# Two-tap filter in the first layer of a block compressor, with the prompt queries kept in DRAM meanwhile

## The reference

```python
CMP_BLOCK = 32; CMP_STRIDE = 16; CMP_HIDDEN = 128; HD_B = 64; N_KV_B = 2

def compress_blocks(kv, pe, w1, w2):
    B, L = kv.shape[:2]
    nseg = L // CMP_STRIDE
    r = CMP_BLOCK // CMP_STRIDE
    n_cmp = nseg - r + 1
    segs = kv[:, :nseg * CMP_STRIDE].reshape(B, nseg, CMP_STRIDE, 2, N_KV_B, HD_B)
    blocks = jnp.concatenate([segs[:, j:j + n_cmp] for j in range(r)], axis=2)
    blocks = blocks + pe.transpose(1, 0, 2)[:, :, None, :]
    flat = blocks.transpose(0, 1, 3, 4, 2, 5).reshape(B, n_cmp, 2, N_KV_B, CMP_BLOCK * HD_B)
    hid = jax.nn.gelu(jnp.einsum('bnkgf,kfh->bnkgh', flat, w1))
    return jnp.einsum('bnkgh,khd->bnkgd', hid, w2)
```

## Time and profile before

| | |
|---|---|
| median of 3 runs | 2916.55 us (2914.92 to 2917.1) |
| profiled execution | 2917.17 us, its span 2915.4 us |
| PE busy | 2804.9 us (96%), 21195 matmul records |
| PE weight loads busy | 2672.6 us (92%) |
| DVE busy | 1190.1 us (41%) |
| ACT busy | 625.0 us (21%) |
| POOL busy | 1008.8 us (35%) |
| mean granted PE clock | 0.986 |

### The profile page before, as it was taken

One profiled execution on the slowest core, in us unless ns is written; L12 is line 12 of the kernel. 1 busy time (PEld: TensorE's weight loads), 2 busy tenths in 40 slices (PEclk: granted clock), 3 DMA queues, 4 the chain that ended last, 5 costly groups with the idle time before them and its releaser, 6 DMA issues.

```text
span 2915.4 us, 49271 instructions
## 1 busy us (share of the span) xinstructions
PE 2804.9 (96%) x21195; PEld 2672.6 (92%) x21195; DVE 1190.1 (41%) x1244; ACT 625.0 (21%) x1092; POOL 1008.8 (35%) x484
## 2 busy tenths in 40 slices
PE   7999989999898799999999999999999999999998
PEld 7999878876776599999999999999999999999998
DVE  5121273345543215444334444416335434444345
ACT  4100044546665302000110001211111110001102
POOL 6342100100002444444344444533554434444340
PEclk9999999989999899999999999999999999999999
DMA  5111243200103531111111111311211111111111
GB/s 182 45 45 49 87 138 94 90 31 2 74 2 131 174 109 44 51 44 44 50 43 50 43 45 48 123 38 50 93 39 52 44 51 43 47 46 43 50 50 58
DMA packets 204235, 185.46 MB, mean 64 GB/s; under 512 B 8013, under 2 KB 185426, under 8 KB 202362
## 3 DMA queue, kind: packets, MB, share of 16 engines
q1 hardware_dynamic: 193290, 160.28, 17.6%
q0 software_dynamic: 4608, 16.78, 1.5%
q10 hardware_dynamic: 6192, 6.29, 0.8%
HBM read 162.41 MB, written 25.09 MB: 64 GB/s over the span
## 4 chain that ended last, share of the span: by engine, by line
PE 79%; issue 8%; DVE 6%; ACT 2%; POOL 2%; DMA 2%; SPq 0%; POOLq 0%; DVEq 0%; ACTq 0%
PE psum L266 49%; PE psum L476 6%; PE psum L298 5%; PE psum L1484 4%; PE psum L1890 2%; PE psum L286 2%; DVE xlo L338 2%; PE psum L1864 2%; POOL whl L237 1%; PE psum L1827 1%; PE psum L1468 1%; DMA wrow<-in_state_win_kv 1%; POOL whl L240 1%; DVE nmax L1993 1%; PE psum L313 1%
## 5 line engine op out<-in xcount | busy, mean ns | idle before, releaser
L266 PE MATMUL psum<-xhi,whl 128*128 128x344 f32 x4656 | 864.0, 320 | 1.3 <-ACT vCs L692 0.6
L237 POOL TENSOR_TENSOR whl<-wraw,zeroc 128x1024 fp32r<-128x1024 f32 x186 | 372.9, 2005 | 1172.2 <-PE psum L266 815.1
L266 PEld LDWEIGHTS psum<-xhi,whl 128*128 128x128 f32 x4656 | 756.2, 188 | 2.3 <-issue 2.1
L240 POOL TENSOR_TENSOR whl<-wraw,whl 128x1024 fp32r<-128x1024 f32 x186 | 501.6, 2697 | 14.6
L266 PE MATMUL psum<-xlo,whl 128*128 128x344 f32 x2328 | 494.1, 321 | 0.0
L266 PE MATMUL psum<-ahi,whl 128*128 128x344 f32 x2304 | 427.5, 320 | 0.2
L266 PEld LDWEIGHTS psum<-xlo,whl 128*128 128x128 f32 x2328 | 394.1, 189 | 0.0
L266 PEld LDWEIGHTS psum<-ahi,whl 128*128 128x128 f32 x2304 | 373.2, 188 | 4.4 <-DVE ftmp L558 3.7
L545 DVE CAST ahi<-frel 128x1032 fp32r<-128x1032 f32 x64 | 170.7, 2667 | 476.3 <-ACT frel L522 475.8
L520 ACT ACTIVATE frel<-psum 128x1032 f32<-128x1032 f32 x64 | 66.1, 1033 | 1231.9 <-PE psum L266 1190.0
L558 DVE TENSOR_TENSOR ftmp<-psum,fscale 128x1032 f32<-128x1032 f32 x127 | 156.3, 1231 | 307.7 <-PE psum L266 247.3
(11 more groups left out here) (430 smaller groups left out, 3062.7 us busy)
## 6 DMA issues: line engine op xcount, KB each, us to landing
wraw<-in_w_ffn SPq DMA_DIRECT2D x128, 512.0 KB, 3.8
rows<-in_cache_cmp_kv SPq DMA_DIRECT2D x128, 128.0 KB, 2.5
wraw<-in_w_in_ab SPq DMA_DIRECT2D x26, 512.0 KB, 3.7
hT<-h_spill SPq DMA_DIRECT2D x8, 1032.0 KB, 8.1
wraw<-in_w_in_c SPq DMA_DIRECT2D x16, 512.0 KB, 3.9
h_spill<-hT SPq DMA_DIRECT2D x4, 1032.0 KB, 8.3
h_spill<-hT SPq DMA_DIRECT2D x1, 4128.0 KB, 12.9
wrow<-in_state_win_kv SPq DMA_DIRECT2D x4, 1024.0 KB
```

Source lines behind the costliest of these rows:

```text
L237: pool.tensor_tensor(whl[:, s, 0, :], raw, zeroc[:, 0:1].to_broadcast([P, UNIT]), ALU.add).then_inc(w_hi, 1)
L240: pool.tensor_tensor(whl[:, s, 1, :], raw, whl[:, s, 0, :].bitcast(F32), ALU.subtract).then_inc(w_ready, 1)
L266: last = pe.matmul(psum[:, 3 * bset + c, 0:TC], w, rhs[ah][:, k0 + k, c * TC:(c + 1) * TC], start=(k == 0 and n == 0), stop=(k == kn - 1 a ...
```

## The change

Pair the blocks. With e[m] = x[2m], o[m] = x[2m+1], block 2m is A e[m] + B o[m] and block 2m+1 is A o[m] + B e[m+1]. The changed kernel computes P[m] = (A + B) o[m] once, and

- block 2m = A (e[m] - o[m]) + P[m],
- block 2m+1 = B (e[m+1] - o[m]) + P[m].

Each `half(x)` has now 24 products of 128 columns (66 for the prompt) where it had 16 of 254 (130). In detail:

- POOL makes the sums of weights `wab` once, and zeroes the difference tiles.
- `differences(eng, x)` makes the two differences of each group after `pairs`, 2 instructions of 248 to 264 elements for each of a half's groups: POOL for x = 0 to 5, DVE for x = 6 to 17. `half(x)` starts with the eight products of A + B and waits for the differences before its ninth (the prompt's halves before their first).
- `joined(x)` on DVE copies P out of PSUM and adds it to both other results, writing `hid`: 3 instructions. `gelu(x)` now works on `hid` in place and waits for `joined` (`m_hp`) instead of PE (`m_h`).
- `xp` is now two tiles with three planes. The first lies where `qB` was. So SP stores `qB` to DRAM (`q_spill`, 2.11 MB) after the input projection's last weight fetch and ahead of the first stores of `kvst`, and reads it back after `half(16)`, 256 columns of each head first. The attention waits for them.
- Three semaphores of the old code are replaced by the chain semaphores that exist.

```diff
+            sp.wait_ge(a_ps, 16)
+            sp.dma_start(q_spill, qB[:, :, :].rearrange("p h t -> p (h t)")).then_inc(q_mv, 16)
...
-        xp = at("xp", R_X + H, [P, 4, SEQ])
+        xp = [at("xp0", R_G + 3 * H, [P, 3, 8, 2, 64]), at("xp1", R_X + H, [P, 3, 8, 2, 64])]
+        wab = [at("wab0", R_G + 3 * H + 12288, [P, 8, P]), at("wab1", R_X + H + 12288, [P, 8, P])]
...
-        hid = at("hid", R_H + 29536, [P, 2, 2 * NCMP_S])
+        hid = at("hid", R_H + 29536, [P, 2, 2, 128])
...
+        p2s = at("p2s", R_H + 32096, [P, 2, 64])
...
+        MADE_ONCE = 4
+
+        def made(x):
+            return MADE_ONCE + 2 * (half_groups(x)[-1][0] + 1)
+
+        def pairs_of(x):
+            return 33 if x < 2 else 64
+
+        def differences(eng, x):
+            c, k = divmod(x, 2)
+            even, odd, diff = xp[k][:, 0, :, :, :], xp[k][:, 1, :, :, :], xp[k][:, 2, :, :, :]
+            for gi, h, g in half_groups(x):
+                eng.wait_ge(m_xp, gi + 1)
+                lo, hi = (0, 31) if h == 0 else (31, 63)
+                eng.tensor_tensor(diff[:, :, g, lo:hi], even[:, :, g, lo + 1:hi + 1], odd[:, :, g, lo:hi], ALU.subtract)                    .then_inc(m_df, 1)
+                eng.wait_ge(m_df, MADE_ONCE + 2 * gi + 1)
+                m = slice(32 * h, 32 * h + (33 if c == 0 else 32))
+                eng.tensor_tensor(even[:, :, g, m], even[:, :, g, m], odd[:, :, g, m], ALU.subtract).then_inc(m_df, 1)
...
             pool.wait_ge(unit_done, AB_END)
+            pool.wait_ge(q_mv, 16)
+            for k in range(2):
+                pool.memset(xp[k][:, 2, :, :, :], 0.0).then_inc(m_df, 1)
+            pool.wait_ge(m_w, 48)
+            for k in range(2):
+                pool.tensor_tensor(wab[k][:, :, :], w1c[:, k, 0:8, :], w1c[:, k, 8:16, :], ALU.add).then_inc(m_df, 1)
+            pool.wait_ge(m_pv, 4)
+            pool.wait_ge(m_df, MADE_ONCE)
+            for x in range(5):
+                differences(pool, x)
             pool.wait_ge(g_sst, 16)
             pool.wait_ge(g_so, 1)
             hv = hatt[:, :, 0:SEQ].rearrange("p h (c t) -> p c h t", t=P)
             pool.memset(hv[:, :, :, 0:64], 0.0).then_inc(g_z, 1)
+            differences(pool, 5)
...
+            def joined(x):
+                c, k = divmod(x, 2)
+                n = pairs_of(x)
+                dve.wait_ge(m_h, x + 1)
+                if c >= 1:
+                    dve.wait_ge(m_o, c)
+                both = psum[:, 2 + k, 256:384].rearrange("p (g m) -> p g m", g=2)[:, :, 0:n]
+                s, v = link("dve", dve.tensor_copy(p2s[:, :, 0:n], both))
+                dve.wait_ge(s, v)
+                for z in range(2):
+                    own_ = psum[:, 2 + k, 128 * z:128 * z + 128].rearrange("p (g m) -> p g m", g=2)[:, :, 0:n]
+                    dst = hid[:, k, :, :].rearrange("p g (m z) -> p z g m", z=2)[:, z, :, 0:min(n, 64)]
+                    ins = dve.tensor_tensor(dst, own_, p2s[:, :, 0:n], ALU.add)
+                    if z == 0:
+                        link("dve", ins)
+                ins.then_inc(m_hp, 1)
...
                 update(l, 0)
+                if l >= 3:
+                    joined(l - 3)
                 place(l, 2)
                 place(l, 3)
...
+            joined(4)
...
+            dve.wait_ge(m_df, made(5))
+            differences(dve, 6)
+            joined(5)
...
+                differences(dve, 7 + c)
+                joined(6 + c)
             gated(NT - 1)
+            differences(dve, 15)
+            joined(14)
             outputs(6)
             permute(NB, 0)
             permute(NB, 1)
+            differences(dve, 16)
+            joined(15)
             dve_keys(dve)
+            differences(dve, 17)
+            joined(16)
             outputs(7)
             dve_keys_low(dve)
+            joined(17)
             outputs(8)
...
-                    act.activation(xp[:, 2 * k + g, :].rearrange("p (e n) -> p e n", e=8)[:, :, 64 * half:64 * half + 64],
-                                   psum[:, gi % 2, :].rearrange("p (n e) -> p e n", e=8), ACT.Copy)\
+                    act.activation(xp[k][:, 0:2, :, g, 32 * half:32 * half + 32],
+                                   psum[:, gi % 2, :].rearrange("p (m z e) -> p z e m", z=2, e=8), ACT.Copy)\
                         .then_inc(m_xp, 1)
...
-                act.wait_ge(m_h, x + 1)
+                act.wait_ge(m_hp, x + 1)
                 if c == 0:
-                    act.activation(hbias[:, k:k + 1], psum[:, 2 + k, 64:65], ACT.Copy).then_inc(m_be, 1)
-                    act.wait_ge(m_be, k + 1)
-                    src = psum[:, 2 + k, 0:130].rearrange("p (g n) -> p g n", g=2)[:, :, 0:n]
-                else:
-                    act.wait_ge(m_o, c)
-                    src = psum[:, 2 + k, 0:2 * n].rearrange("p (g n) -> p g n", g=2)
-                act.activation(hid[:, k, 0:2 * n].rearrange("p (g n) -> p g n", g=2), src, ACT.Gelu_apprx_tanh,
+                    s, v = link("act", act.activation(hbias[:, k:k + 1], hid[:, k, 0, 64:65], ACT.Copy))
+                    act.wait_ge(s, v)
+                act.activation(hid[:, k, :, 0:n], hid[:, k, :, 0:n], ACT.Gelu_apprx_tanh,
                                bias=hbias[:, k:k + 1]).then_inc(m_hg, 1)
...
+            act.wait_ge(q_mv, 16)
...
-                n = NCMP_P + 2 if c == 0 else NCMP_S
+                n = pairs_of(x)
                 follow = half_groups(x + 1) if x + 1 < HALVES else []
                 pe.wait_ge(m_xp, half_groups(x)[-1][0] + 1)
-                if c >= 1:
-                    pe.wait_ge(m_hg, x - 1)
-                xv = xp[:, 2 * k:2 * k + 2, :].rearrange("p g (e n) -> p g e n", e=8)
-                o = psum[:, 2 + k, 0:2 * n].rearrange("p (g n) -> p g n", g=2)
+                if c == 0:
+                    pe.wait_ge(m_df, made(x))
+                else:
+                    pe.wait_ge(m_hp, x - 1)
+                terms = ((256, wab[k], 0, 1), (0, w1c[:, k, :, :], 0, 0), (128, w1c[:, k, :, :], 8, 2))
                 for q in range(4):
-                    for j in range(4 * q, 4 * q + 4):
-                        s = j // 8
-                        last = pe.matmul(o, w1c[:, k, j, :], xv[:, :, j % 8, s:s + n], start=(j == 0), stop=(j == 15))
+                    for i in range(6 * q, 6 * q + 6):
+                        c0, weights, first, operand = terms[i // 8]
+                        j = i % 8
+                        if i == 8:
+                            pe.wait_ge(m_df, made(x))
+                        o = psum[:, 2 + k, c0:c0 + 128].rearrange("p (g m) -> p g m", g=2)[:, :, 0:n]
+                        last = pe.matmul(o, weights[:, first + j, :], xp[k][:, operand, j, :, 0:n],
+                                         start=(j == 0), stop=(j == 7))
                     if q == 3:
                         last.then_inc(m_h, 1)
...
+            q_back = q_spill.rearrange("p (h t) -> p h t", h=NH)
+            sp.wait_ge(q_mv, 16)
+            sp.wait_ge(m_h, 17)
+            sp.dma_start(qB[:, :, 0:2 * P], q_back[:, :, 0:2 * P]).then_inc(q_mv, 16)
+            sp.dma_start(qB[:, :, 2 * P:T], q_back[:, :, 2 * P:T]).then_inc(m_kn, 16)
...
+            if i == 2:
+                act.wait_ge(m_kn, 32)
...
             pe.wait_ge(m_cm, 2)
+            pe.wait_ge(q_mv, 32)
```

30 lines of the change are left out of this document (16 added, 14 removed).

## The result

The changed kernel took 2923.05 us (median of 20 runs, 2913.34 to 2929.49), the kernel before 2916.57 us (median of 20, 2910.74 to 2919.45). The ratio is 1.0022, with a 95% interval of 1.0016 to 1.0028: slower. The forecast was 2915.6, with 0.48 for no change and 0.30 for slower. Its range of 2908 to 2928 holds the median, but the sign and the reason are missed: I expected 0.9 us less and 6.5 us more came. That the range holds it is partly luck: the levels cost 15.8 us more than forecast, and some 9 us came back behind the stage, where I had nothing.

What follows compares the result with a forecast made beforehand. The prediction took PE to bound the chunk loop and DVE to be fuller at 380 to 400 us. Against 2917.2 us it summed 5.5 + 8.0 - 19.2 + 4.8 = -0.9, giving 2916.3, or 2915.6 as median; range 2908 to 2928.

Steps and rivals of the forecast that it cites:

- which is what the half saves: Levels 4 and 5: PE's wait for sample_state grows by 1.5 us, as much as the half saves; sum 0.1 us.
- PE's products: Compressor halves: 0.112 us a record, saving 1.48 us for each of 16 halves; half(0) of the prompt 1.6 us longer.
- The store: Queries stored ahead of the kvst stores on the same queue: 5.5 us more, all on the path; upper bound 6.4.
- the low clock behind the stop is there now and I leave it as it is: After PE's stop for the kvst stores: the existing stretch at 1.2 GHz stays unchanged, no cost added.
- So I add 2.5 for a stretch at 1.2 GHz: Level 3, after PE's 3.6 us idle before the first sample's transposes: low clock costs 2.5 us.
- Levels together: 8.0 us more: Levels 3 to 7: 5.2 late at level 4, 2.5 for low clock, 0.3 for later levels.
- half(4)'s 1.5 us are spent waiting for: Level 6: later store of sample states delays POOL's memset to 454.3, absorbing half(4)'s saving; 0.2 us more with it.
- POOL: Levels: weight sums by 378, half(0)'s differences by 382, about 0.7 us per instruction of 256 elements; off the path.
- The loop and the stage's end: Halves 5 to 17 save 19.2 us; four places at the end of the stage give back 4.8 us.
- Every new stop drops the clock: Rival, chance 0.13: stops in levels 4, 5 and half(15) each bring 2 us of low-clock cost; 2921 us.
- DVE never bounded the loop: Rival, chance 0.17: differences from about 0.7 us make DVE the chunk loop's bound, losing 12 us; 2928 us.
- the save per record was not smaller: Rival, chance 0.1: records take 0.119 us, the switch's pace, adding 4.3 us over 13 halves; 2919 us.

Runs made afterwards that it cites:

- e5: Changed kernel with the new products only from half(6) on, halves 0 to 5 as before, queries stored early among the weight fetches: 2892.9 us, 0.9927 of the kernel before.
- e1: Kernel before with only the late store of the queries to DRAM and their way back added: 2923.4 us, 1.0024 of the kernel before.
- e6: Changed kernel plus 60 products with overwritten results, filling PE's stops in half(1), half(2) and half(3): 2914.7 us, 1.0003 of the kernel before.
- e4: Changed kernel with the first GELU moved on ACT behind the permutation of the first sample's rows: 2916.9 us, 0.9998 of the kernel before.
- e9: Changed kernel with the new products only up to half(5), 16 products a half from half(6) on: 2941.8 us, 1.0078 of the kernel before.
- e8: Kernel before with the late query store, its way back, and POOL's part of the change on tiles nobody reads: 2921.2 us, 1.0025 of the kernel before.

## Why the prediction was wrong

**What bounds the kernel** was read rightly, and stated: in the levels DVE is the fuller engine (18.93 of 20 us), in the loop PE. The consequence was not drawn. Where PE waits anyway, products that are saved come back as stops. I had this as "which is what the half saves" and costed it at 0.1 and 0.2 us, the time, without the clock.

**PE's products** were right: 0.112 us a record in the loop and 0.113 in the prompt's shape, half(0) 1.6 us longer (391.66 to 397.94 is 6.28, before 4.65), 1.5 us saved per half in the loop (e5: 12.1 for eight). The rule of the Trainium skill (TensorE: Matmul & The Clock Gate, LDWEIGHTS (loading the stationary operand)) that the load takes its columns however few move is borne out by the 66-column records: 24 in 397.94 - 395.22 = 2.72 us, 0.113 each.

**The store**: forecast 5.5. DVE's wait grew by 4.8, the projection's end by 4.0; over the whole kernel it is 6.2 (e1). Right in size, by luck in part: the wait grew less than I took it, and "the low clock behind the stop is there now and I leave it as it is" was wrong. The low stretch behind the stop grew (the sum over 290 to 322 us is 5.1 instead of 3.4), and e1's profile has one in level 2 that the kernel before has not.

**The levels are the step that failed**: "So I add 2.5 for a stretch at 1.2 GHz", and with it "Levels together: 8.0 us more". Measured were 23.8. The stop itself was forecast well (3.49 for 3.6), its wake not: I had sized it by one row, 32 records behind 459.20, as if the clock came back within some 4 us. It stayed at 0.50 for some 20 us, 10.2 us by the sum over the windows where I had 2.5, and each further stop of 2 us, which I had at nothing, had a wake too. Levels 1 and 2 were at nothing as well and cost 4.2 us. The kernel before had such a long stretch too, 617 to 633 us, which I had not looked at, and one of 3.4 us in level 6 without a stop. e6 shows that the stops are the cause of most of it, e4 that it needs no 3.5 us stop, e5 and e9 that all of it belongs to the levels. Why the clock stays low for 20 us behind one stop and for 3.4 behind another is open.

**Level 6.** "half(4)'s 1.5 us are spent waiting for" POOL's memset did not come true: the memset ended at 479.5, and ACT wrote `hatt` only from 481.93. half(4)'s saving is gone all the same (27.5 us late at level 6, 27.8 at half(5)), and the longer low stretch behind 470 us lies there.

**POOL** was said to be off the path at 0.7 us a difference and weights by 378. The weights landed for it only at 377.8 and it took 6.73 us for the two sums, and DVE beside it lost up to 2.1 us on one instruction; some 3.2 of the 23.8 us (e8). The Trainium skill says as much (GPSIMD Engine Reference, 1. Specifications): POOL shares its SBUF interfaces with VectorE, in contention with DVE instructions in a two-port mode or with two SBUF inputs. The trace agrees: the updates with two SBUF inputs took up to 3.36 instead of 1.22 us, and the masked copies from PSUM stayed at 1.32. `kE<-fT` of level 0, with one SBUF input, took 3.64 instead of 2.36 beside POOL's memset; whether it runs in the two-port mode no trace shows.

**The loop and the stage's end**: forecast -19.2 + 4.8 = -14.4, measured 12.2 - 27.8 = -15.6. Two of the waits at the end can be read directly, 1.58 us before the transposes of the last sample's rows and 2.81 before the last second layer (1.7 more than the earlier trace rows, as said).

**Behind the stage** I had nothing, and some 9 us came back in the profiled pair: the long low stretch at the attention's start of the kernel before (about 5), and one wait for the sample stage's rows instead of two (15.63 us against 12.76 and 3.73), with less low clock behind it (about 4). How much of it the other runs have can't be told; by the means the change is 7.1 us slower than the kernel before beside it (2923.0 against 2915.9).

**The rivals.** "Every new stop drops the clock" was the one that came nearest, with 0.13, and priced by the same wrong row, 2 us a stop. DVE never bounded the loop (differences mostly 0.43), and the save per record was not smaller (by its own sum that rival stands at 2919.9, not 2919).
